# Three float32r products per weight tile become one float32 product, weights used from a ring of six buffers

## The reference, cut to what matters

```
xn   = rmsnorm(x)
proj = xn @ w_in                     # 1024 x 5632: zu, zv, q, k, va, ga, gb
u, v = gelu(zu), gelu(zv)
y_a  = spatial_gating(u, v) @ w_branch_a      # 1024 x 1024
y_b  = sliding_window_attention(q, k, va) @ w_branch_b   # 1024 x 1024
h    = x + (sigmoid(ga)*y_a + sigmoid(gb)*y_b) @ w_out   # 1024 x 1024
out  = rmsnorm(h + mixture_of_experts(rmsnorm(h)))       # 32 experts, top 2 of one group
```

## Time and profile before

| | |
|---|---|
| median of 3 runs | 1037.84 us |
| the runs | 1037.84, 1035.43, 1037.91 us |
| span of the profiled execution (first to last instruction) | 1034.2 us |
| TensorE matmul busy in it | 958.9 us, 93% |
| VectorE busy | 489.2 us, 47% |
| ScalarE busy | 269.6 us, 26% |
| GpSimd busy | 25.0 us, 2% |
| read from HBM | 244.50 MB |
| chain that ended last, by engine | TensorE 89%, VectorE 6% |

### The profile page before, as it was taken

One profiled execution on the slowest core, in us unless ns is written; L12 is line 12 of the kernel. 1 busy time (PEld: TensorE's weight loads), 2 busy tenths in 40 slices (PEclk: granted clock), 3 DMA queues, 4 the chain that ended last, 5 costly groups with the idle time before them and its releaser, 6 DMA issues.

```text
span 1034.2 us, 13947 instructions
## 1 busy us (share of the span) xinstructions
PE 958.9 (93%) x5675; PEld 624.5 (60%) x5675; DVE 489.2 (47%) x918; ACT 269.6 (26%) x427; POOL 25.0 (2%) x25
## 2 busy tenths in 40 slices
PE   3999999999999999593599999999999999999993
PEld 3888888777777888482454455554545545455442
DVE  3636335766672444258643443443443424434335
ACT  5323223644442211125121112120111211121102
POOL 0000000000000000005000000000000000000001
PEclk9999999999999999897699999999999999999997
DMA  8353222122115446834297999999999979999942
GB/s 285 82 111 93 86 78 82 42 82 71 52 57 138 132 120 229 282 127 163 107 364 323 387 395 388 413 402 390 394 383 413 402 268 392 412 387 395 396 155 83
DMA packets 93268, 247.12 MB, mean 239 GB/s; under 512 B 22168, under 2 KB 45744, under 8 KB 84784
## 3 DMA queue, kind: packets, MB, share of 16 engines
q1 hardware_dynamic: 90528, 245.90, 63.6%
q10 hardware_dynamic: 2704, 0.71, 0.3%
HBM read 244.50 MB, written 2.10 MB: 238 GB/s over the span
## 4 chain that ended last, share of the span: by engine, by line
PE 89%; DVE 6%; issue 1%; ACTq 1%; ACT 1%; DMA 1%; SPq 0%; DVEq 0%; POOL 0%; POOLq 0%
PE bank L730 22%; PE bank L755 11%; PE bank L714 9%; PE bank L504 9%; PE bank L506 9%; PE bank L505 9%; PE bank L767 3%; PE bank L768 3%; PE bank L531 3%; PE bank L533 3%; PE bank L532 2%; PE bank L565 2%; ACTq L900 1%; PE bank L741 1%; DMA x_tok<-x 1%
## 5 line engine op out<-in xcount | busy, mean ns | idle before, releaser
L730 PE MATMUL bank<-W,packT 128*64 128x512 f32 x1024 | 226.8, 595 | 2.9 <-issue 2.9
L730 PEld LDWEIGHTS bank<-W,packT 128*64 128x64 f32 x1024 | 74.1, 137 | 132.6 <-issue 131.6
L1017 DVE TENSOR_TENSOR wlo<-raw,whi 128x2048 fp32r<-128x2048 f32 x34 | 77.7, 2288 | 100.4 <-ACT whi L805 100.3
L504 PE MATMUL bank<-xnT_hi,whi 128*128 128x512 f32 x288 | 113.7, 395 | 0.8 <-DVE wlo L1017 0.8
L755 PE MATMUL bank<-W,actT 128*64 128x512 f32 x512 | 113.4, 595 | 0.0
L506 PE MATMUL bank<-xnT_hi,wlo 128*128 128x512 f32 x288 | 112.2, 390 | 0.0
L505 PE MATMUL bank<-xnT_lo,whi 128*128 128x512 f32 x288 | 112.2, 389 | 0.0
L714 PEld LDWEIGHTS bank<-onehot,hn_part 128*128 128x128 bf16 x1632 | 95.0, 99 | 25.0 <-issue 24.8
L714 PE MATMUL bank<-onehot,hn_part 128*128 128x128 bf16 x1632 | 101.9, 222 | 7.6 <-DVE onehot L1311 7.6
L1364 DVE SCALAR_TENSOR_TENSOR y_lo<-bank,small,y_hi 128x512 fp32r<-128x512 f32 x32 | 24.0, 751 | 145.4 <-ACT y_hi L970 145.4
L805 ACT ACTIVATE whi<-raw 128x2048 fp32r<-128x2048 f32 x34 | 64.8, 1909 | 87.5 <-PE bank L506 30.2
(11 more groups left out here) (231 smaller groups left out, 1193.5 us busy)
## 6 DMA issues: line engine op xcount, KB each, us to landing
W<-w_up SPq DMA_DIRECT2D x32, 2048.0 KB, 11.2
W<-w_down SPq DMA_DIRECT2D x64, 1024.0 KB, 12.6
W<-w_gate SPq DMA_DIRECT2D x30, 2048.0 KB, 12.0
raw<-w_in SPq DMA_DIRECT2D x18, 1024.0 KB, 5.1
raw<-w_in SPq DMA_DIRECT2D x16, 256.0 KB, 4.4
raw<-w_branch_a SPq DMA_DIRECT2D x4, 1024.0 KB, 4.9
raw<-w_branch_b SPq DMA_DIRECT2D x16, 256.0 KB, 4.6
raw<-w_out SPq DMA_DIRECT2D x4, 1024.0 KB, 5.1
```

The costliest lines, as they stand in the source:

```text
L504: pe.matmul(dst, hi_w, hi_x, start=start, stop=False)
L730: mm = pe.matmul(dst[s * ROWS:(s + 1) * ROWS, :], packT[:, c, s * ROWS:(s + 1) * ROWS], W[u][:, c * DE:(c + 1) * DE], start=(c == 0), stop ...
L1017: dve.tensor_tensor(wlo[c % 2][:, :], raw[c % 2][:, :], whi[c % 2][:, :].bitcast(F32), ALU.subtract).then_inc(lo_split, 1)
```

## The change

- The weights are multiplied as float32 straight from the buffer into which they were loaded. `split_hi`, `split_lo`, `start_unit`, `whi`, `wlo` and their semaphores are gone.
- The three float32r matmuls of a product become one float32 matmul.
- The 48 KB of `raw`, `whi` and `wlo` become a ring of six buffers of 8 KB a partition. Unit c goes to buffer c mod 6, and the last four units to buffers 4, 5, 2 and 3. A load waits until TensorE has used the unit that was in its buffer.
- All 34 units are now loaded ahead of the first experts' weights.
- The activations have one float32 copy each. ScalarE writes the even and VectorE the odd blocks of `xnT`. VectorE no longer makes the rests of `spT`, `attT` and `mgT`. The factor 0.5 of `mgT` moves into the addition of `h`.

```diff
-    raw = [at(f"raw{b}", [P, 2048], F32, 128 + 8 * b) for b in range(2)]
-    whi = [at(f"whi{b}", [P, 2048], F32R, 144 + 8 * b) for b in range(2)]
-    wlo = [at(f"wlo{b}", [P, 2048], F32R, 160 + 8 * b) for b in range(2)]
+    ring = [at(f"ring{b}", [P, 2048], F32, 128 + 8 * b) for b in range(RING)]
...
+        LAST_SLOTS = {30: 4, 31: 5, 32: 2, 33: 3}
+
+        def slot(c):
+            return LAST_SLOTS.get(c, c % RING)
...
             def load_unit(c):
-                if c >= 2:
-                    sp.wait_ge(hi_split, c - 1)
-                    sp.wait_ge(lo_split, c - 1)
+                if before[c] is not None:
+                    wait_unit_used(sp, before[c])
                 for dst, src in units[c]:
-                    sp.dma_start(dst, src).then_inc(unit_loaded[c % 2], 16)
+                    sp.dma_start(dst, src).then_inc(unit_loaded[slot(c)], 16)
...
-            for c in range(2, UNITS - 2):
+            for c in range(2, UNITS):
                 load_unit(c)
-                if c == GB + 3:
+                if c == GB + 6:
                     sp.wait_ge(att_ready, STEPS // 2)
                     sp.dma_start(h_tok[:, :, :], ...)
             wait_unit_used(sp, WO - 2)
             load_experts(0, w_gate, 0, 1)
-            load_unit(UNITS - 2)
             wait_unit_used(sp, WO - 1)
             sp.wait_ge(merged_ready, KT)
             load_experts(2, w_up, 0, 1)
-            load_unit(UNITS - 1)
             load_down(0, 1)
...
-            def wide_unit(c, kh, xT_hi, xT_lo, done, before_last=None):
+            def wide_unit(c, kh, xT, done, before_last=None):
 
-                pe.wait_ge(lo_split, c + 1)
+                pe.wait_ge(unit_loaded[slot(c)], landed[c])
...
-                        pe.matmul(dst, xT_hi[:, kk, ts], w_h[:, k, :], start=first, stop=False)
-                        pe.matmul(dst, xT_hi[:, kk, ts], w_l[:, k, :], start=False, stop=False)
-                        mm = pe.matmul(dst, xT_lo[:, kk, ts], w_h[:, k, :], start=False, stop=last)
+                            pe.wait_ge(xnT_odd if kk % 2 else xnT_even, kk // 2 + 1)
+                        mm = pe.matmul(bank[t][:, :], xT[:, kk, t * P:(t + 1) * P], w[:, k, :],
+                                       start=(kh == 0 and k == 0), stop=(kh == 1 and k == WIDE - 1))
...
             def tall_tile(c, m, dst, xT, done):
 
                 if m == 0:
-                    pe.wait_ge(lo_split, c + 1)
+                    pe.wait_ge(unit_loaded[slot(c)], landed[c])
...
                 for k in range(KT):
-                    mm = three(dst, w_h[:, k, ms], w_l[:, k, ms], xT_hi[:, k, :], xT_lo[:, k, :],
-                               k == 0, k == KT - 1)
+                    mm = pe.matmul(dst, w[:, k, m * P:(m + 1) * P], xT[:, k, :], start=(k == 0), stop=(k == KT - 1))
...
-                    then(dve.tensor_tensor(merged[:, :], merged[:, :], branch_a[:, j, :], ALU.add))
-                    then(dve.tensor_scalar(mgT_hi[:, j, :], merged[:, :], 0.5, None, ALU.mult))
-                    dve.scalar_tensor_tensor(out=mgT_lo[:, j, :], ...)
+                    dve.tensor_tensor(mgT[:, j, :], merged[:, :], branch_a[:, j, :], ALU.add).then_inc(merged_ready, 1)
...
-                dve.tensor_tensor(part, bank[t][:, :], part, ALU.add).then_inc(h_ready, 1)
+                dve.scalar_tensor_tensor(out=part, in0=bank[t][:, :], scalar=0.5, in1=part, op0=ALU.mult,
+                                         op1=ALU.add).then_inc(h_ready, 1)
```

More of the change, by code:

```diff
@@ L58, in build_block @@
     FAR_PAIRS = PAIRS - 6
+    RING = 6
     MAX_OV = SEQ // ROWS - 1
@@ L70, in at @@
         return nc.alloc_sbuf_tensor_at(name, shape, dt, offset=base + int(kb * KB))
-    xnT_hi = at("xnT_hi", [P, KT, SEQ], F32R, 0)
-    xnT_lo = at("xnT_lo", [P, KT, SEQ], F32R, 16)
+    xnT = at("xnT", [P, KT, SEQ], F32, 0)
     v_tok = at("v_tok", [P, TT, D], F32, 32)
-    attT_hi = at("attT_hi", [P, KT, SEQ], F32R, 32)
-    attT_lo = at("attT_lo", [P, KT, SEQ], F32R, 48)
+    attT = at("attT", [P, KT, SEQ], F32, 32)
     dist_i = at("dist_i", [P, BAND], I32, 48)
@@ L90, in build_block @@
     xn_tok = at("xn_tok", [P, TT, D], F32, 112)
[L91 to L94, removed]
-    raw = [at(f"raw{b}", [P, 2048], F32, 128 + 8 * b) for b in range(2)]
-    whi = [at(f"whi{b}", [P, 2048], F32R, 144 + 8 * b) for b in range(2)]
-    wlo = [at(f"wlo{b}", [P, 2048], F32R, 160 + 8 * b) for b in range(2)]
+    spT = at("spT", [P, KT, SEQ], F32, 112)
+    mgT = at("mgT", [P, KT, SEQ], F32, 96)
+    ring = [at(f"ring{b}", [P, 2048], F32, 128 + 8 * b) for b in range(RING)]
     kT = at("kT", [P, 2, SEQ], F32, 176)
@@ L188, in build_block, with unit_view @@
         units = []
-        def raw_view(c, kt):
-            return raw[c % 2][:, :].rearrange("p (k n) -> p k n", k=kt)
+        LAST_SLOTS = {30: 4, 31: 5, 32: 2, 33: 3}
+        def slot(c):
+            return LAST_SLOTS.get(c, c % RING)
+        def unit_view(c, kt):
+            return ring[slot(c)][:, :].rearrange("p (k n) -> p k n", k=kt)
         def add_unit(kt, moves):
             c = len(units)
-            units.append([(dst(raw_view(c, kt)), src) for dst, src in moves])
+            units.append([(dst(unit_view(c, kt)), src) for dst, src in moves])
         whole = lambda v: v
@@ L236, in build_block @@
         UNITS = len(units)
-        landed = []
+        assert UNITS == 34
+        landed, before = [], []
         for c in range(UNITS):
-            landed.append((landed[c - 2] if c >= 2 else 0) + 16 * len(units[c]))
+            same = [b for b in range(c) if slot(b) == slot(c)]
+            before.append(same[-1] if same else None)
+            landed.append((landed[same[-1]] if same else 0) + 16 * len(units[c]))
         x_loaded, x_reloaded = [sem(f"x_loaded{t}") for t in range(TT)], sem("x_reloaded")
@@ L244, in build_block @@
         consts_loaded, late_loaded = sem("consts_loaded"), sem("late_loaded")
-        unit_loaded = [sem("unit_loaded0"), sem("unit_loaded1")]
-        hi_split, lo_split = sem("hi_split"), sem("lo_split")
+        unit_loaded = [sem(f"unit_loaded{b}") for b in range(RING)]
         half_used = sem("half_used")
@@ L251, in build_block @@
         normed_low, normed_high = sem("normed_low"), sem("normed_high")
-        xnT_psum, xhi_ready, xnT_ready = (sem(n) for n in ("xnT_psum", "xhi_ready", "xnT_ready"))
+        xnT_psum, xnT_even, xnT_odd = (sem(n) for n in ("xnT_psum", "xnT_even", "xnT_odd"))
         act_tile_done, act_tile_read = sem("act_tile_done"), sem("act_tile_read")
@@ L500, in _ @@
                 mm.then_inc(xnT_psum, 1)
[L502 to L506, removed]
-            def wide_unit(c, kh, xT_hi, xT_lo, done, before_last=None):
-                pe.wait_ge(lo_split, c + 1)
-                w_h = whi[c % 2][:, :].rearrange("p (k n) -> p k n", k=WIDE)
-                w_l = wlo[c % 2][:, :].rearrange("p (k n) -> p k n", k=WIDE)
+            def wide_unit(c, kh, xT, done, before_last=None):
+                pe.wait_ge(unit_loaded[slot(c)], landed[c])
+                w = unit_view(c, WIDE)
                 for t in range(TT):
@@ L537, in wide_unit, with tall_tile @@
                     mm.then_inc(half_used, 1)
-            def tall_tile(c, m, dst, xT_hi, xT_lo, done):
+            def tall_tile(c, m, dst, xT, done):
                 if m == 0:
-                    pe.wait_ge(lo_split, c + 1)
-                w_h = whi[c % 2][:, :].rearrange("p (k n) -> p k n", k=TALL)
-                w_l = wlo[c % 2][:, :].rearrange("p (k n) -> p k n", k=TALL)
-                ms = slice(m * P, (m + 1) * P)
+                    pe.wait_ge(unit_loaded[slot(c)], landed[c])
+                w = unit_view(c, TALL)
                 for k in range(KT):
-                    mm = three(dst, w_h[:, k, ms], w_l[:, k, ms], xT_hi[:, k, :], xT_lo[:, k, :],
-                               k == 0, k == KT - 1)
+                    mm = pe.matmul(dst, w[:, k, m * P:(m + 1) * P], xT[:, k, :], start=(k == 0), stop=(k == KT - 1))
                 mm.then_inc(done, 1)
@@ L553, in act_tile @@
                 pe.wait_ge(act_tile_read, a - 1)
-                tall_tile(c, m, bank[a % 2][:, :], xnT_hi, xnT_lo, act_tile_done)
+                tall_tile(c, m, bank[a % 2][:, :], xnT, act_tile_done)
             def attention_slot(s):
@@ L601, in _ @@
             for c in range(ZV, Q):
-                wide_unit(c, c % 2, xnT_hi, xnT_lo, act_tile_done)
+                wide_unit(c, c % 2, xnT, act_tile_done)
                 if c == 1:
@@ L638, in _ @@
                     if u == 0 and m == 0:
-                        pe.wait_ge(sp_ready, KT)
+                        pe.wait_ge(gate_used, KT)
                     d = 2 * u + m
                     pe.wait_ge(gate_used, 8 + d)
-                    tall_tile(GA + 2 * u + 1, m, bank[2][:, :], spT_hi, spT_lo, dve_tile_done)
+                    tall_tile(GA + 2 * u + 1, m, bank[2][:, :], spT, dve_tile_done)
                     attention_slot(5 + 4 * u + m)
@@ L652, in _ @@
```

(17 more changed lines are left out.)

39 lines of the change are left out of this document (2 added, 37 removed).

## The result

The changed kernel takes 1117.72 us (median of 4 runs, 1117.33 to 1118.47). The kernel before takes 1036.78 us (median of 4, 1035.43 to 1037.91). The ratio is 1.078, with a 95% interval of 1.0765 to 1.0795: 81 us slower. The forecast was 1121, range 1110 to 1148. The profiled execution took 1117.64 us, with a span of 1115.8 us.

The account below looks back on a forecast made before the run. The prediction took TensorE to bound the rewritten stage, busy 400.4 of 401.5 us. Its terms: 1034.2 + 97.0 - 10.8 - 1.5 - 1.1 = 1117.8 us span, plus 3.6 carried over to the median: 1121 us, range 1110 to 1148.

Parts of the forecast that it names:

- The bound: Stage rewritten by the diff: TensorE is the bound, busy 400.4 of 401.5 us, with 1.1 us idle to give back.
- The product, +97.0: 544 products on TensorE: two float32 records of 0.4292 us replace three float32r of 0.2267, 370.0 to 467.0 us.
- The ceiling of 0.453: Upper limit in us of a float32 record's step: two present float32r steps, making the products +122.9 us.
- The weight loads, 0: TensorE's products: each weight load, about 0.19 us, hides under the matmul before it and adds nothing.
- the third rival: TensorE's products: weight loads not hidden, each of 1088 adding 0.188 us, 204.5 us in all: 1325 us; chance 4%.
- The hole, -10.8: In w_out, TensorE's wait at L531 for wlo, behind ScalarE's slow router-load issues, goes: 10.8 us less.
- its clock, -1.5: After TensorE's wait in w_out, eight steps at the 1.2 GHz level took 3.28 us, not 1.81: 1.5 us less.
- The idle rest, -1.1: TensorE's remaining idle time before 421.5 us goes: at most 1.1 us less.
- The start, 0: First product, at 23.47 us right after the transposes: halving the work on xnT gives 0.
- What was costed at 0: Landings, reload of x, extra starting loads, add_h and ScalarE's router-load issues of about 13 us: each adds 0.
- the sum: Whole kernel's profiled span: 1034.2 + 97.0 - 10.8 - 1.5 - 1.1 = 1117.8 us.

Follow-up runs that it names:

- router_early: Kernel before, with four of the five router loads issued by ScalarE after the attention, in the branch-b stage: 1023.82 us, ratio 0.9876.
- split_first: Kernel before, with the split of unit 31 moved on ScalarE ahead of the router's loads: 1027.55 us, ratio 0.992.

## Why the prediction was right

**The bound.** Right. TensorE had 1.1 us to give back before the hole; all other freed time, 100 us of VectorE and 60 of ScalarE, bought nothing.

**The product, +97.0.** Right, and this was the step that could have gone otherwise. The step was carried from records with half as many stationary columns; it came out at 0.4292 us, 1088 x 0.4292 = 467.0. A pair of half-width records had taken, side by side, the same 0.4292 us as one full-width record does. L627 had given the structure (two passes plus a small fixed part), and the run with half the columns confirmed it at a second size. The ceiling of 0.453 rested on carrying float32r's 0.0134 us to each pass; that part is paid once a record, and only by float32r.

**The weight loads, 0.** A load of 0.190 us on the same rows lies under the matmul ahead of it at steps of 0.4292 and of 0.216 us, so the third rival falls. The Trainium skill (TensorE: Matmul & The Clock Gate, section "The mechanism", where the line that the forecast cites stands) says that a weight load overlaps a running matmul only when it goes to another row group, and above that line that a load into a background weight buffer is pulled ahead too. The line does not hold for the records of these runs. The text above it fits them, but no run shows which way the array took.

**The hole, -10.8, and its clock, -1.5.** Right in size and in cause, now shown: moving the loads' issue gave 12.5 us on the kernel before; the old load order gave nothing back on the kernel after. The forecast named two causes in one breath (loads ahead of the experts, no split behind ScalarE). Only the second mattered: in `router_early` the loads keep their old order and no product waits for a split behind the branches.

**The idle rest, -1.1.** It went: TensorE is busy 527.52 of 527.52 us.

**The start, 0.** It was -0.3 us.

**What was costed at 0.** The landings, the ring, the order of the loads and `add_h` were all 0. One zero had less cover than I gave it: ScalarE's issues of the router's loads did not take 13 us but 27, and the wait of VectorE for their landing ended only as TensorE's next tile was done, with nothing to spare. The forecast took the duration from a trace in which two loads of 2 MB had just been issued; after the change there were four, and four of 1 MB behind them.

**The sizes that were off.** The span came out 2.0 us below the sum (1115.8 for 1117.8). In the first stretch it is 82.25 for 83.6: 1.3 us, whose cause stays open. The changes of type between plain float32 and float32r are gone, but they cost nothing to speak of. The eight records of L627 start at 139.64 us, so at 0.111 us each the first float32r record is due at 140.53; it starts at 140.45, 0.08 early, and its successor (140.76) follows after 0.31 us instead of 0.227, 0.08 late. The two cancel. The start gave 0.3, routing and experts together 0.4. A further 1.7 us is what lies around the span: 1.84 us in the profiled run, where I had carried over 3.6 from a median and a span of different executions. Together with the rounding of the forecast that is its 3.3 us.

## What to carry to other kernels

Price a precision change by the step of one product, not by its instruction count: three float32r records (0.680 us) beat two plain float32 ones (0.858 us) here although they need splits, and the splits were worth removing only where they ended a wait. When a hole closes together with a large rewrite, try to close it alone: here the place of four small loads in ScalarE's queue was worth 12.5 us by itself, and the rewrite hid it. Before spending freed time of a covered engine on new work, count the slack within one unit of the loop, not over the stage.

## What the runs showed of the hardware that I had not expected

- The issue of a small load can hold its engine for many microseconds while large loads are under way. Four issues took 2.4 us in the branch-b stage, where the DMA engines were busy 46% of the time (357 to 360 us of `router_early`). That of `b_router<-b_router_group` took 8.56 us beside the experts' two up loads of 2 MB, 10.27 in `split_first`, where SyncE was also issuing the four down loads of 1 MB, and 17.55 in the changed kernel, where four loads of 2 MB had just been issued and the four of 1 MB were being issued. In all three the DMA engines were busy throughout. What such an issue waits for was not taken apart. ScalarE stands still for that long:

```profile
498.65 17.55 ACTq L854 DMA_DIRECT2D b_router<-b_router_group  x1
516.23 7.58 ACTq L854 DMA_DIRECT2D b_router<-b_router_expert  x1
```

- A float32r record costs 0.0134 us over its columns at 2.4 GHz, at 256 columns as at 512, and a plain float32 record with its two passes under 0.003 us. With 1632 records that is 22 us of the kernel before. What it is was not found.
